# The end of a fused two-block transformer kernel in token layout: y starts as x turned, gates folded into biases and expert outputs, final norm along rows, one outer branch

## The reference, cut to what matters

```python
x = x + gate1 * _mixer(h, ...)
h = _rmsnorm(x, norm2_w[l]) * (1.0 + scale2) + shift2
x = x + gate2 * _moe(h, ...)
return _rmsnorm(x, final_norm_w)
```

## Time and profile before

| | |
|---|---|
| three runs | 2747.04, 2750.99 (median), 2752.54 us |
| the profiled execution | 2751.5 us, its span 2749.5 us |
| mean granted TensorE clock | 0.973 |
| busy, share of the span | PE 95%, DVE 53%, ACT 36%, POOL 1% |
| read from HBM over the span | 703.62 MB |

### The profile page before, as it was taken

How to read it: one execution, slowest core, us unless ns; L and a number is a source line. 1 busy time by engine, 2 the same in 40 slices (tenths; PEclk the granted TensorE clock), 3 DMA queues, 4 the chain that set the end, 5 groups by cost and what they waited for, 6 DMA issues and landing times.

```text
span 2749.5 us, 49286 instructions
## 1 busy us (share of the span) xinstructions
PE 2607.9 (95%) x19500; PEld 2111.8 (77%) x19501; DVE 1453.0 (53%) x2614; ACT 989.8 (36%) x1683; POOL 30.6 (1%) x21
## 2 busy tenths in 40 slices
PE   7999999999899999999989979999999999999996
PEld 6999699999899869999968869855555555555553
DVE  5666676666666666666656875433333333333333
ACT  4444454444444445444334434412121121121121
POOL 0000000000000000000000210000000000000000
PEclk9999999999999999999999989999999999999997
DMA  8644544444455464544443224499999999999994
GB/s 262 236 181 167 222 149 182 169 180 182 159 183 183 161 253 150 184 166 182 179 161 138 93 92 151 177 428 430 430 430 430 430 430 430 430 430 430 430 430 182
DMA packets 70344, 708.89 MB, mean 258 GB/s; under 512 B 10983, under 2 KB 11239, under 8 KB 13239
## 3 DMA queue, kind: packets, MB, share of 16 engines
q1 hardware_dynamic: 65144, 699.30, 63.5%
q0 software_dynamic: 5088, 8.05, 1.4%
HBM read 703.62 MB, written 3.67 MB: 257 GB/s over the span
## 4 chain that ended last, share of the span: by engine, by line
PE 85%; DVE 6%; ACT 5%; issue 2%; DMA 1%; DVEq 0%; SPq 0%; ACTq 0%
PE ps L2025 16%; PE ps L1526 15%; PE ps L1529 15%; PE ps L1530 15%; PE ps L2050 6%; PE ps L2008 4%; ACT xg L833 3%; PE ps L2063 2%; PE ps L1557 1%; PE ps L2035 1%; PE ps L1561 1%; PE ps L1560 1%; DVE u_lo L913 1%; DMA slot<-in_experts 1%; ACT u_hi L481 1%
## 5 line engine op out<-in xcount | busy, mean ns | idle before, releaser
L913 DVE TENSOR_TENSOR u_lo<-ring,u_hi 128x1024 fp32r<-128x1024 f32 x500 | 615.9, 1237 | 464.5 <-ACT u_hi L481 461.0
L481 ACT ACTIVATE u_hi<-ring 128x1024 fp32r<-128x1024 f32 x498 | 523.9, 1057 | 692.7 <-PE ps L1526 641.3
L1526 PE MATMUL ps<-hs,u_hi 128*128 128x256 f32 x2408 | 694.6, 288 | 24.2 <-DVE hs L939 22.3
L1529 PE MATMUL ps<-hs,u_hi 128*128 128x256 f32 x2408 | 687.8, 286 | 0.0
L1530 PE MATMUL ps<-hs,u_lo 128*128 128x256 f32 x2408 | 687.5, 286 | 0.0
L1526 PEld LDWEIGHTS ps<-hs,u_hi 128*128 128x128 f32 x2408 | 468.5, 195 | 35.2 <-DVE hs L939 21.3
L2025 PE MATMUL ps<-slot,xg 128*64 128x256 f32 x4096 | 466.6, 381 | 10.5 <-ACT xg L833 10.4
L1529 PEld LDWEIGHTS ps<-hs,u_hi 128*128 128x128 f32 x2408 | 469.3, 195 | 0.5
L1530 PEld LDWEIGHTS ps<-hs,u_lo 128*128 128x128 f32 x2408 | 468.8, 195 | 0.0
L2025 PEld LDWEIGHTS ps<-slot,xg 128*64 128x64 f32 x4096 | 294.5, 137 | 220.8 <-issue 91.3
L2050 PE MATMUL ps<-slot,eact 128*64 128x512 f32 x1024 | 250.0, 609 | 4.0 <-DMA slot<-in_experts 3.6
(11 more groups left out here) (340 smaller groups left out, 3046.2 us busy)
## 6 DMA issues: line engine op xcount, KB each, us to landing
slot<-in_experts SPq DMA_DIRECT2D x256, 1536.0 KB, 18.7
ring<-in_stream SPq DMA_DIRECT2D x184, 1536.0 KB, 6.4
slot<-in_experts SPq DMA_DIRECT2D x4, 1024.0 KB, 5.0
bias<-bias_rows POOLq DMA_DIRECT2D x2, 1280.0 KB, 11.4
konst<-in_konst POOLq DMA_DIRECT2D x1, 2272.0 KB, 14.5
bias_rows<-vecs POOLq DMA_DIRECT2D x3, 512.0 KB, 13.8
x_tok<-in_x SPq DMA_DIRECT2D x1, 1024.0 KB, 5.4
bias_rows<-vecs POOLq DMA_DIRECT2D x1, 1024.0 KB, 62.4
```

Source lines behind the costliest of these rows:

```text
L481: nc.scalar.activation(u_hi[buffer_of(l, k)][:, :], raw_unit(l, k), ACT.Copy).then_inc(unit_hi, 1)
L913: nc.vector.tensor_tensor(u_lo[b][:, :], raw_unit(l, kk), u_hi[b][:, :].bitcast(F32), ALU.subtract).then_inc(unit_lo, 1)
L1526: mm = mm_(dst, hi, x_hi, start=first, stop=False, skip_group_check=True)
L1529: mm_(dst, hi, x_lo, start=False, stop=False, skip_group_check=True)
```

## The change

- **y begins as x turned.** DVE copies the turned x from banks 2 to 5 to `y_tok` (`copy_xtok`, four copies), two of them before the logits and two before the first expert. `turn_x(1)` moves ahead of the logits. ACT's first `take_htok` also waits for the first two copies.
- **Gates.** POOL makes two diagonal matrices (of gate2 and of the final norm's weight, 128x1024 each), after the last projection. PE multiplies ones by them, which gives a 128-row copy of each vector in PSUM. ACT copies that of gate2 to `gate_rows` and `gate_half`; POOL multiplies the expert biases `bout` by `gate_rows`. DVE makes `outd` as expert output times `gate_half` (ACT's `take_out` goes). The bias sums wait for `bout_scaled` and are added to `y_tok` by DVE (ACT's four copies go).
- **xg** is made by two DVE instructions of 128x512 instead of eight on ACT.
- **Last expert.** `back` uses banks 6, 7, 2 and 5, so its second half no longer waits for additions. The rows of the final norm's weight are made by PE before the last expert's steps 2 and 3, and copied by ACT.
- **Branch.** A register loaded before the experts says whether any further pass is needed; the loop over passes stands within one `If`.
- **End.** ACT squares and sums the rows of one token half, DVE those of the other; ACT takes the root of 128x2 values, DVE the reciprocal, and DVE makes each half's output in place, in one instruction of 128x1024; SP stores each half in a DMA of its own.
- The wait for `cols_landed` becomes one for `konst1_landed`, and the router's totals and turned weights both use bank 1, so the latter wait for `total_taken`.

```diff
         def _(sp):
...
+            again = sp.value_load(flags[0:1, 1:2], min_val=0, max_val=1)
+            with sp.If(again > 0):
+                with sp.Fori(1, PASSES) as p:
...
+            for t in range(TT):
+                sp.wait_ge(out_made, t + 1)
+                sp.dma_start(out[t * P:(t + 1) * P, :], y_tok[:, t, :]).then_inc(stored, 16)
...
         def _(pool):
...
+            pool.wait_ge(out_ready, LAYERS * OUTS + OUTS)
+            for i, col in enumerate((mod[:, 5 * DC:6 * DC], cols[:, C_NF:C_NF + DC])):
+                pool.tensor_tensor(diag[i][:, :, :], ident.unsqueeze(1).to_broadcast([P, DC, P]), col.unsqueeze(2).to_broadcast([P, DC, P]),
+                                   ALU.mult).then_inc(diag_ready, 1)
+            pool.wait_ge(rows_taken, 2)
+            pool.tensor_tensor(bout, bout, gate_rows[:, :], ALU.mult).then_inc(bout_scaled, 1)
...
         def _(a):
...
             a.wait_ge(rstd_ready, Q + 3)
+            a.wait_ge(xtok_copied, 2)
             take_htok(0)
...
-            def take_tokens(n, b):
-
-                a.wait_ge(xg_ready, n + 1)
-                for c in range(DC):
-                    op = nc.scalar.activation(xg[:, b, c, :], ps[:, 2, c * CAP:(c + 1) * CAP], ACT.Identity,
-                                              scale=modgain[:, DC + c:DC + c + 1], bias=mod[:, 3 * DC + c:3 * DC + c + 1])
-                op.then_inc(xg_taken, 1)
+            a.wait_ge(rows_ready, 2)
+            for i, bank in enumerate((0, 7)):
+                nc.scalar.activation(gate_rows[:, i * 512:(i + 1) * 512], ps[:, bank, :], ACT.Copy).then_inc(rows_taken, 1)
+            for i, bank in enumerate((0, 7)):
+                part = slice(i * CAP, (i + 1) * CAP)
+                nc.scalar.activation(gate_half[part, :], ps[part, bank, :], ACT.Copy).then_inc(rows_taken, 1)
...
+            nc.scalar.activation(small[:, 36:37], one_col, ACT.Sqrt)
+            a.wait_ge(y_made, 1)
+            nc.scalar.activation(squared[:, :], y_tok[:, 0, :], ACT.Square, accum_out=ysum[:, 0:1]).then_inc(ssum_ready, 1)
+            a.wait_ge(ssum_ready, Q + 5)
+            nc.scalar.activation(ystd, ysum, ACT.Sqrt, bias=eps_col[EPS2], scale=1.0 / D).then_inc(std_ready, 1)
...
         def _(v):
...
+            copy_xtok(0)
+            copy_xtok(1)
             v.wait_ge(logit_ready, 1)
...
+            def take_tokens(p, e, b, after_first=True):
...
+                v.wait_ge(xg_ready, n + 1)
+                moe(nc.vector.tensor_tensor(xg[:, b, :, :], ps[:, 2, 0:DC * CAP].rearrange("p (a b) -> p a b", b=CAP),
+                                            modgain[:, DC:2 * DC].unsqueeze(2).to_broadcast([P, DC, CAP]), ALU.mult))
+                nc.vector.tensor_tensor(xg[:, b, :, :], xg[:, b, :, :], mod[:, 3 * DC:4 * DC].unsqueeze(2).to_broadcast([P, DC, CAP]),
+                                        ALU.add).then_inc(xg_taken, 1)
...
                     for r in (2 * j, 2 * j + 1):
                         add_output(n - 1, e - 1, r)
+                if j == 1 and not last:
+                    take_tokens(p, e + 1, 1 - b)
+                if j == PAIRS - 1:
+                    v.wait_ge(moe_used, n * DC + DC)
+                    nc.vector.tensor_tensor(outd[:, :], ps[:, 4, :], gate_half[:, :], ALU.mult).then_inc(eout_taken, 1)
...
+            v.drain().then_inc(y_made, 1)
+            v.wait_ge(y_made, 1)
+            nc.vector.tensor_tensor_reduce(h_tok[:, 1, :], y_tok[:, 1, :], y_tok[:, 1, :], 1.0, 0.0, ALU.mult, ALU.add, ysum[:, 1:2]).then_inc(ssum_ready, 1)
+            v.wait_ge(rows_taken, 6)
+            v.wait_ge(std_ready, Q + 4)
+            nc.vector.reciprocal(yrec, ystd).then_inc(rstd_ready, 1)
+            v.wait_ge(rstd_ready, Q + 4)
+            for t in range(TT):
+                nc.vector.scalar_tensor_tensor(out=y_tok[:, t, :], in0=y_tok[:, t, :], scalar=yrec[:, t:t + 1], in1=norm_rows[:, :], op0=ALU.mult,
+                                               op1=ALU.mult).then_inc(out_made, 1)
...
         def _(pe):
...
             turn_x(0)
+            turn_x(1)
             pe.wait_ge(x_ready, (Q + 2) * OUTS + 4)
...
+            pe.wait_ge(diag_ready, 1)
+            rows(0, 0, 0)
+            rows(0, 1, 7)
             pe.wait_ge(sel_ready, 1)
...
-                else:
+                elif banks == (6, 7):
                     pe.wait_ge(scat_added, n * (2 * TT) + 2 * t)
...
                 expert_turn(p, EXPERTS - 2, 0, last=True)
+                if isinstance(p, int):
+                    pe.wait_ge(diag_ready, 2)
+                    rows(1, 0, 2)
+                    rows(1, 1, 5)
                 expert_step(p, EXPERTS - 1, 2, 1, last=True)
                 expert_step(p, EXPERTS - 1, 3, 1, last=True)
+                pe.wait_ge(rows_taken, 6)
                 for t in range(TT):
-                    back(n + (EXPERTS - 1), t, 1)
+                    back(n + (EXPERTS - 1), t, 1, LAST_BANKS[t])
```

More of the change, by code:

```diff
@@ L59 @@
 PASSES = TOK // CAP
[L60 removed]
+LAYER_STEPS, MOE_STEPS = 50, 2 * PAIRS + 1
 ALPHA, LIMIT = 1.702, 7.0
@@ L1471, in expert_pass @@
                 n = p * EXPERTS
+                take_tokens(p, 0, 0, after_first=False)
+                if isinstance(p, int):
+                    for i in range(2 * TT):
+                        v.wait_ge(bias_sums_ready, i + 1)
+                        ys = y_tok[:, i // 2, i % 2 * 512:i % 2 * 512 + 512]
+                        nc.vector.tensor_tensor(ys, ys, ps[:, BIAS_BANKS[i], :], ALU.add).then_inc(ybias_taken, 1)
                 v.wait_ge(placeT_ready, n + 1)
                 find_places(1)
-                expert_step(p, 0, 0, after=False)
@@ new lines, in expert_pass @@
+                expert_turn(p, EXPERTS - 2, 0, places=False, last=True)
+                expert_step(p, EXPERTS - 1, 2, 1, places=False, last=True)
+                expert_step(p, EXPERTS - 1, 3, 1, last=True)
+                for r in range(2 * TT):
+                    add_output(n + (EXPERTS - 1), EXPERTS - 1, r, LAST_BANKS[r // 2])
+            v.wait_ge(flags_ready, 1)
+            again = v.value_load(flags[0:1, 1:2], min_val=0, max_val=1)
+            for i in range(2, 2 * TT):
+                v.wait_ge(htok_taken, i + 1)
+                copy_xtok(i)
@@ new lines, in _ @@
+            assert before_experts == step.base + step.k
+            expert_pass(0)
+            with v.If(again > 0):
+                with v.Fori(1, PASSES) as p:
+                    needed = v.value_load(flags[0:1, bass.ds(p, 1)], min_val=0, max_val=1)
+                    with v.If(needed > 0):
+                        moe.base, moe.k = before_experts + p * (EXPERTS * MOE_STEPS + 1) - 1, 0
+                        v.wait_ge(placeT_ready, p * EXPERTS)
+                        moe(nc.vector.tensor_scalar(rank[:, :, :], rank[:, :, :], -float(CAP), None, ALU.add))
+                        find_places(0)
+                        expert_pass(p)
@@ L1984, in _, with rows @@
             mm.then_inc(logit_ready, 1)
-            for i in range(1, 2 * TT):
+            for i in range(2, 2 * TT):
                 turn_x(i)
+            def rows(i, half, bank):
+                mm_(ps[:, bank, :], ones, diag[i][:, half * 4:half * 4 + 4, :], start=True, stop=True).then_inc(rows_ready, 1)
+            pe.wait_ge(diag_ready, 1)
+            rows(0, 0, 0)
+            rows(0, 1, 7)
             pe.wait_ge(sel_ready, 1)
@@ L2009, in gather @@
                 mm.then_inc(xg_ready, 1)
-                if not first:
+                if first:
+                    pe.wait_ge(xtok_copied, 2 * TT)
+                else:
                     pe.wait_ge(placeT_taken, n)
```

180 lines of the change are left out of this document (76 added, 104 removed).

## The result

The changed kernel took 2722.78 us (median of four runs, 2718.28 to 2726.31), the kernel before, beside it, 2750.04 us (four runs): ratio 0.990, 95% interval 0.9882 to 0.9919. A repeat with more runs gave 2724.39 against 2748.07 us, ratio 0.9906, 0.9893 to 0.9920. So it is faster by some 24 to 27 us. The profiled execution took 2726.31 us, its span 2724.6 us, so the profiled pair is 24.9 us apart (2749.5 - 2724.6).

The account below looks back on a forecast made before the run. The weight stream over DMA, slower than PE by a hair, bounds the loop; stages before and after it count fully. Span 2749.5 - 21.9 (end) + 0.1 (before experts) = 2727.7, execution 2729.7, forecast 2729.2 us, range 2723 to 2734.

Parts of the forecast that it names:

- The branch: End, after the additions: the new `If` keeps the 2.74 us wait behind the first taken branch, plus 0.1.
- the four calls of `back`: End: four calls without a wait, 2 x 2.10 us; DVE's last addition ends 0.70 behind; 2.1 us saved.
- row sums: End: ACT's squares and DVE's product and sum side by side, 1.3 us with hand-over; bounds 1.1 and 2.5.
- root and reciprocal: End: root 0.26 us, reciprocal of two columns and two hand-overs 0.3 us.
- store: End: second half's 0.52 MB lands after 2.8 us, the first half out of its way; bounds 2.0 and 4.0.
- Worth 0: Loop of experts: moving xg and `outd` to DVE gains nothing, since PE then waits for DMA instead.
- Rivals 3 and 4: Loop: bound by PE, 2719 us, chance 0.04; DVE's new operations get into PE's turn, 2782 us, chance 0.03.
- `rows(0)` on PE, two matmuls: Before the experts: falls into PE's wait for `sel`, from 1760.56 until DVE finishes the top 4; cost 0.
- Rival 2: Routing: `rows(0)` fills PE's idling and the clock stays at 2.4 GHz, speeding gather and bias sums; 2725 us, chance 0.15.
- the 0.2 for contention: Before the experts: POOL's diagonals delay DVE's two-SBUF-input L1394 by some 0.5 us, mostly covered; 0 to 0.5, taken 0.2.
- `L1394` delayed: Sign, before the experts: this DVE operation is held by POOL's diagonals to about 1760.4.
- the second `expert_in` ending at 1783.2: Sign, start of the loop: it ends within 0.5 us of 1783.2, so the stages before the experts hardly move.

Follow-up runs that it names:

- four more fillers: Changed kernel plus four 128x512 matmuls with unused results, three ahead of `rows(0)`, one before the wait for the turned weights: 2721.09 us.
- xg on ACT: Changed kernel with xg made by ACT in eight instructions again for all experts, DVE doing a dummy operation instead: 2723.24 us, ratio 0.9902.
- all nine runs: The changed kernel's four first runs and the five of its repeat, nothing altered: median 2723.46 us.
- short last tiles: Changed kernel with SP's last four transfers cut to the 0.5 MB each for `expert_out`: 2717.01 us; with the four idle-time matmuls also added: 2715.88 us.

## Why the forecast was right on the end and the loop, and wrong on the routing

**The end, right.** Forecast a saving of 21.9, measured 22.5. From the last product's end to the span's end the forecast has 16.15 us, the profile 15.55. The branch took 1.0 less than forecast (1.60 for 2.74 of wait), the four calls of `back` with their additions took 0.3 more. The forecast let the last addition end 0.70 behind PE, but both additions of a half stand behind it, 1.40 us, as the earlier trace rows already had it (2717.86, x2); PE's eight records took 3.80 for 4.20. (The 0.55 of "issue" between the last two additions in the chain is no idle time: DVE is busy with the first of them, as its timeline shows.)

```profile
2713.70 1.41 DVE L1447 SCALAR_TENSOR_TENSOR y_tok<-ps,wt,y_tok 128x512 f32<-128x512 f32 x2 [0.29 <-PE ps L2120]
```

The smaller terms came as forecast: row sums 1.23 for 1.3, root and reciprocal 0.62 for 0.56, two halves 2.48 for 2.46, store 2.7 for 2.8. The three parts undone cost a little less than the sum had for them: the branch 3.3 to 3.6 (in the sum 7.1 - 2.8 = 4.3), the banks 1.7 to 2.0 (2.1), the split store 0.8 to 1.1 (1.2).

**The loop, right.** "Worth 0", with PE waiting for DMA: its turn 28.66 (forecast 28.9), 925.74 us of stream (forecast within 2 of 926). Rivals 3 and 4, a PE-bound loop and DVE in PE's turn, are out.

**The routing, wrong, and this is the step that failed:** "`rows(0)` on PE, two matmuls, falls into PE's wait for `sel` [...] Cost 0." The cost was 0; the gain, 2.6 us, was left out, so that the sum before the experts had +0.1 us where -2.7 came. I had asked what the work costs, and had bounded that from both sides, but priced the idle time that it fills at nothing, though the clock of 0.66 and the gather of 7.06 stood in my rows. Rival 2 named the mechanism and got 0.15, on the ground that "two matmuls are little". They are not little beside a wait of 1.99 us: they took 1.88. (The nearest row, four 512-column records of `back` in 2.10, was taken at half clock and on 64 partitions, so it was a rough guide at best.) Rival 2's price was for a clock that stays high throughout, 4 us; what came is the half-way case. The full one came with four more fillers, 4.4 us (27.70 to 23.27) with their own 1.3 us paid, and once without them (23.10, xg on ACT). Filling the wait is one way to the gain and not the only one: with the same two matmuls on the path and the wait open, the stage took 24.60. And the place of the fall, which the forecast let vary from execution to execution, was the same to 0.2 us in all eight profiles with the wait filled in which it came.

The other terms ahead of the experts: POOL's diagonals took 1.90 each, not 2.42, and were done at 1760.09, before DVE's L1410 at 1760.70, so the 0.2 for contention was 0 (x to gather 9.61 in both). The scaled biases were ready at 1769.43, forecast 1769.5. Of the signs that the forecast set down, three did not come: the wait of 2.7 behind the branch (1.60), `L1394` delayed (L1410 started 0.76 us later, as x did), and the second `expert_in` ending at 1783.2 (1781.27).

**The number.** 2729.2 - 2722.78 = 6.4 us. Routing 2.8 (2.7 and the 0.1 that was expected as a loss), end 0.6, stream 0.4 make 3.8. The other 2.6 are scatter of executions: the profiled one came 0.75 later to the routing, had 0.3 less outside its span, and stands 3.5 above its median, where I had carried over the 0.5 of the kernel before (3.0 + 0.3 - 0.75 = 2.6). The range ended 0.2 above the median that came: it had room for rival 2 or for the scatter, not for both in the same direction. That the median came 0.2 outside and not inside is chance: the repeat's 2724.39 and the 2723.46 of all nine runs lie inside. The 2.7 us missing from the routing are not.

**Still open:** why the wait behind the first taken branch is 2.73 to 2.76 in the three kernels without an outer branch, and 1.00 to 1.76 in the ones with it; no run separates the length of the jump from what else differs there. And why the clock did not fall in one routing with the changed kernel's work on PE.

## What to carry to other kernels

Ask of each piece of work moved into an idle stretch of PE not only what it costs but what the idle stretch had cost behind it: here 2 us of idling were followed by 13.7 us at half clock, and two 128x512 matmuls, useful or not, bought back 2.6 us of a stage where every microsecond counts. A whole time that scatters by 10 us doesn't show this; the stage of a profile does. A wait taken out of a loop that a transfer stream holds comes back as a wait for the stream; in such a loop the bytes are what to look at, and 4 MB too many at its end were worth some 6 us, a part of it by the clock of a PE that no longer waits. In such a comparison the half clock at the end of a kernel counts too: `back` took 3.80 us there and 1.99 at full clock. In a serial tail add the operations up one by one: that sum was right within 0.6 of 22 us.

## What the runs showed of the hardware that I had not expected

- Two 128x512 matmuls ahead of the gather, mostly at the low clock and on the path (3.06 us), made the stage no longer (24.60 for 24.98): the low clock lasted 3.4 us instead of 6.8.
- POOL's product of two broadcast inputs, 128x1024, took 1.90 us; of dense inputs 2.42 in the earlier trace rows, 2.36 for the biases.
- In the routing the clock fell 8.2 to 8.3 us behind the last addition to x in three kernels in which PE had stood idle for 2.0 to 2.4 us, and 11.6 to 11.8 us in seven in which that wait was filled; the low stretch was 6.8 us in all of the seven.
- The wait behind a taken branch was 2.73 to 2.76 us in three kernels, 1.43 to 1.76 in eight with an outer `If`, and 1.00 in the two with the short last tiles; the jumped-over bodies are almost the same.
- Two stores of 512 KB, issued 1.2 us apart, landed in 2.7 us each, one of 1 MB in 4.0.
